# Projections of k and of the first half of q, issued in steps of three matmuls between the indexer's matmuls

## What is computed

```
h = rms_norm(x) * (1 + scale) + shift              # scale, shift from c @ ada_w
z = h @ w_in                                       # columns: u | q | k | v | qi | ki | wi
score = sum_h wi[h] * relu(qi[h] . ki) / const     # indexer, 8 heads of 64; causal
sel = top_k(score, 128 or 130)                     # keys that a query may see
y_att = softmax(q . k[sel] / 8 + bias) @ v[sel]    # 8 heads of 64
y_pool = windowed means of u, minus u, @ pool_w    # 4 groups of 128 channels
x = x + gate * rms_norm([y_pool, y_att] @ w_out)
x = x + gate * rms_norm(relu(h2 @ w_ff1)^2 @ w_ff2)
```

## Time and profile before

| | us |
|---|---|
| median of 3 runs | 950.38 |
| lowest and highest run | 945.65, 954.45 |
| profiled execution, its time | 945.28 |
| profiled execution, its span | 943.4 |
| TensorE busy | 855.5 |
| VectorE busy | 449.0 |
| ScalarE busy | 335.5 |

### The profile page before, as it was taken

One profiled execution on the slowest core, in us unless ns is written; L12 is line 12 of the kernel. 1 busy time (PEld: TensorE's weight loads), 2 busy tenths in 40 slices (PEclk: granted clock), 3 DMA queues, 4 the chain that ended last, 5 costly groups with the idle time before them and its releaser, 6 DMA issues.

```text
span 943.4 us, 11350 instructions
## 1 busy us (share of the span) xinstructions
PE 855.5 (91%) x4136; PEld 645.3 (68%) x4136; DVE 449.0 (48%) x862; ACT 335.5 (36%) x627; POOL 88.1 (9%) x136
## 2 busy tenths in 40 slices
PE   2799889998987986879988999999999999999997
PEld 0477437887844564435766788888888888888875
DVE  0342899778457873231365532234333433344256
ACT  2453642223355563220356332234212331134232
POOL 2141200006123320001010000000000000000000
PEclk9989799999979897999998999999999999999999
DMA  9742300221367566857201222222232222321202
GB/s 323 267 113 83 98 1 11 90 90 64 116 210 265 178 204 203 232 155 237 77 21 50 85 90 90 86 61 77 90 90 67 68 90 89 90 66 69 90 1 100
DMA packets 68777, 105.82 MB, mean 112 GB/s; under 512 B 6986, under 2 KB 32214, under 8 KB 68714
## 3 DMA queue, kind: packets, MB, share of 16 engines
q1 hardware_dynamic: 64194, 96.48, 32.2%
q0 software_dynamic: 3296, 6.39, 2.3%
q10 hardware_dynamic: 1232, 2.23, 0.7%
HBM read 100.04 MB, written 5.15 MB: 112 GB/s over the span
## 4 chain that ended last, share of the span: by engine, by line
PE 72%; DVE 4%; ACT 2%; issue 2%; DMA 1%; SPq 1%; POOL 0%; DVEq 0%; ACTq 0%
PE bank L745 69%; PE bank L748 3%; DVE probs L1789 1%; ACT stage L1228 1%; DMA raw<-in_ada_w 1%; DVE keys L1602 1%; SPq L545 1%; SPq L563 0%; DVE x_res L1890 0%; DVE act_lo L1602 0%; DMA pages<-in_cache_k 0%; POOL near L689 0%; DMA out_k_p<-stage 0%; ACT pv_rows L1228 0%; DVE probs L1804 0%
## 5 line engine op out<-in xcount | busy, mean ns | idle before, releaser
L745 PE MATMUL bank<-act_hi,w_split 128*128 128x512 f32 (+1 forms) x800 | 258.2, 395 | 1.6 <-DVE k_lo L1602 1.6
L745 PEld LDWEIGHTS bank<-act_hi,w_split 128*128 128x128 f32 (+1 forms) x800 | 150.9, 189 | 35.0 <-issue 2.6
L496 DVE TENSOR_TENSOR w_split<-raw,w_split 128x2048 fp32r<-128x2048 f32 (+2 forms) x47 | 105.0, 2236 | 143.0 <-ACT w_split L1203 142.9
L745 PE MATMUL bank<-w_split,hid_hi 128*128 128x512 f32 x512 | 159.2, 392 | 0.0
L745 PE MATMUL bank<-act_lo,w_split 128*128 128x512 f32 (+1 forms) x400 | 156.9, 392 | 0.0
L1203 ACT ACTIVATE w_split<-raw 128x2048 fp32r<-128x2048 f32 (+2 forms) x48 | 89.3, 1862 | 94.7 <-PE bank L745 94.7
L745 PEld LDWEIGHTS bank<-w_split,hid_hi 128*128 128x128 f32 x512 | 95.9, 188 | 20.7
L745 PE MATMUL bank<-w_split,hid_lo 128*128 128x512 f32 x256 | 100.2, 391 | 0.0
L745 PEld LDWEIGHTS bank<-act_lo,w_split 128*128 128x128 f32 (+1 forms) x400 | 75.5, 189 | 15.5
L1228 ACT ACTIVATE stage<-bank 128x512 f32<-128x512 f32 (+3 forms) x51 | 30.1, 591 | 95.5 <-PE bank L745 92.2
L745 PE MATMUL bank<-w_split,act_s 128*128 128x512 f32 (+1 forms) x248 | 60.7, 387 | 1.5 <-DVE out_t L1896 1.5
(11 more groups left out here) (249 smaller groups left out, 1091.9 us busy)
## 6 DMA issues: line engine op xcount, KB each, us to landing
raw<-in_w_ff SPq DMA_DIRECT2D x32, 1024.0 KB, 5.2
raw<-in_ada_w SPq DMA_DIRECT2D x20, 1024.0 KB, 5.2
raw<-in_w_in SPq DMA_DIRECT2D x10, 1024.0 KB, 5.1
pages<-in_cache_k SPq DMA_DIRECT2D x32, 256.0 KB, 3.0
v_pages<-in_cache_v SPq DMA_DIRECT2D x32, 256.0 KB, 3.1
pages<-in_ada_w SPq DMA_DIRECT2D x4, 1024.0 KB, 12.5
raw<-in_w_out SPq DMA_DIRECT2D x4, 1024.0 KB, 6.3
x_in<-in_x_prompt SPq DMA_DIRECT2D x1, 2048.0 KB, 14.6
```

The source lines that it names most:

```text
L496: return ops.tensor_tensor(lo, r, hi.bitcast(F32), ALU.subtract)
L745: return nc.tensor.matmul(out, lhsT, rhs, start=start, stop=stop, skip_group_check=True)
```

## The change

Three pairs of chunks, k0, k1 and q0, are no longer projected by `project` but by a generator `project_steps`, which yields after every three matmuls. TensorE issues four steps of k0 before the prompt's scores and one behind each of the twelve pairs of heads; k1 and q0 are issued in the decode loop, two steps before and two behind each turning of page keys. The pieces' order becomes k0, k1, q0, u0, u1, q1. The scores of every second pair of heads go to banks 6 and 7 in place of 0 and 1. What was between the projections (history, turned channels, turned keys) finds new places, ScalarE and VectorE take the copies, splits and low parts of the three pairs into their indexer code, and VectorE's 36 steps are cut into four times nine with a low part behind each nine.

```diff
-    p += [("qi", 0), ("qi", 1), ("kiwi", 0), ("k", 0), ("k", 1), ("u", 0), ("u", 1)]
-    p += [("q", 0), ("q", 1), ("v", 0), ("v", 1), ("poolw", 0)]
+    p += [("qi", 0), ("qi", 1), ("kiwi", 0), ("k", 0), ("k", 1), ("q", 0), ("u", 0)]
+    p += [("u", 1), ("q", 1), ("v", 0), ("v", 1), ("poolw", 0)]
...
+    for t in range(1, NT):
+        for h in range(H):
+            take(("ix", t, h), (3 if h // 2 % 2 == 0 else 6) + h % 2)
...
-    for t in range(1, NT):
-        for h in range(H):
-            take(("ix", t, h), (3 if h // 2 % 2 == 0 else 0) + h % 2)
...
+    for kind, i in (("k", 0), ("k", 1), ("q", 0), ("u", 0), ("u", 1), ("q", 1)):
+        take((kind, 2 * i), 0), take((kind, 2 * i + 1), 1), take((kind + "R", i), 2), take((kind + "S", i), 2)
+    for g in range(NG):
+        take(("uo", g), 3 + g % 2)
+    for t in range(NT + 1):
+        take(("kout", t), 5 + t % 2)
...
+            def project_steps(kind, i):
+
+                hi, lo, both = piece(kind, i)
+                for j in range(2):
+                    key, cols = (kind, 2 * i + j), slice(128 * j, 128 * j + 128)
+                    out = claim(key)
+                    for kc in range(KC):
+                        mm(out[:, :], hi[:, kc, cols], act_hi[:, kc, :], kc == 0, False)
+                        mm(out[:, :], hi[:, kc, cols], act_lo[:, kc, :], False, False)
+                        last = mm(out[:, :], lo[:, kc, cols], act_hi[:, kc, :], False, kc == KC - 1)
+                        if kc == KC - 1:
+                            done(last, key)
+                            if j == 0:
+                                fold_pending()
+                            else:
+                                done(rows_s(claim((kind + "R", i))[:, :], both), (kind + "R", i))
+                                pending.append((kind, i))
+                        yield
...
+            first_k = project_steps("k", 0)
...
+            steps(first_k, 2)
...
+            steps(first_k, 1)
...
+            steps(first_k, 1)
...
+                    steps(first_k, 1)
...
+            def more_projections():
+                yield from project_steps("k", 1)
+                yield from project_steps("q", 0)
+
+            beside = more_projections()
...
                 done(mm(claim(("ixS", b))[0:64, :], qi_s[:, b, :], kx_t[:, 512 * (b % 2):512 * (b % 2) + 512], True, True), ("ixS", b))
                 done(mm(claim(("ixSn", b))[0:64, 0:DS], qi_s[:, b, :], ki_s[:, b * DS:(b + 1) * DS], True, True), ("ixSn", b))
+                steps(beside, 2)
                 if b + 1 < DB:
                     turn_kidx(b + 1)
+                steps(beside, 2)
                 if b == 0:
...
-            for i in range(2):
-                project("k", i)
-                if i == 0:
-                    pe.wait_ge(S["hist_in"], 16)
-                    out = claim("hist")
-                    for g in range(NG):
-                        last = turn(out[:, 120 * g:120 * g + 120], hist_in[:, 128 * g:128 * g + 128], 120)
-                    done(last, "hist")
+            project("u", 0)
+            pe.wait_ge(S["hist_in"], 16)
+            out = claim("hist")
+            for g in range(NG):
+                last = turn(out[:, 120 * g:120 * g + 120], hist_in[:, 128 * g:128 * g + 128], 120)
+            done(last, "hist")
+            project("u", 1)
...
-            for i in range(2):
-                project("u", i)
-            project("q", 0)
...
+            def first_channels():
+                evacuated(pe, ("u", 1))
+                evacuated(pe, ("uS", 0))
+                for g in range(2):
+                    turn_channels(g)
+
+            project("q", 1, first_channels)
             evacuated(pe, ("u", 3))
             evacuated(pe, ("uS", 1))
-            for g in range(NG):
-                if g == 2:
-                    fold_pending()
+            for g in range(2, NG):
                 turn_channels(g)
             turn_keys()
-            project("q", 1)
...
             act.wait_ge(S["bias_row_out"], 16)
             for t in range(1, NT):
                 L = 128 * (t + 1)
                 for h in range(H):
                     n = (t - 1) * H + h
+                    if n == 10:
+                        k_chunk(0, full(act, ("k", 0)))
                     out = full(act, ("ix", t, h))
                     if n >= 2:
                         act.wait_ge(S["relu_added"], n - 1)
                     free(run(rows[:, n % 2, 0:L], out[:, 0:L], ACT.Relu, scale=HD ** -0.5), ("ix", t, h))
+            k_chunk(1, full(act, ("k", 1)))
+            pair_rows("k", 0)
...
+                if b == 2:
+                    k_chunk(2, full(act, ("k", 2)))
+                    k_tail(0, full(act, ("kS", 0)))
+                if b == 4:
+                    k_chunk(3, full(act, ("k", 3)))
+                    pair_rows("k", 1)
+                if b == 6:
+                    q_chunk(0, full(act, ("q", 0)))
+                    k_tail(1, full(act, ("kS", 1)))
+            q_chunk(1, full(act, ("q", 1)))
+            pair_rows("q", 0)
+            q_tail(0, full(act, ("qS", 0)))
...
+            pair("u", 0, u_chunk, u_tail)
+            free(run(hist_t, full(act, "hist")[:, 0:480].rearrange("p (g n) -> p g n", g=NG)), "hist")
+            pair("u", 1, u_chunk, u_tail)
+            q_chunk(2, full(act, ("q", 2)))
+            for g in range(2):
+                last_rows(g)
+            q_chunk(3, full(act, ("q", 3)))
+            pair_rows("q", 1)
+            for g in range(2, NG):
+                last_rows(g)
             for t in range(NT + 1):
                 r = rows_of(t)
                 n, ins = stage_copy(full(act, ("kout", t))[0:r, :], r)
@@ -1416,7 +1470,7 @@
                 evacuated(act, ("kout", t))
                 store(n, r, heads(o["k_p"][0, 0, 128 * t:128 * t + 128]) if t < NT
                       else o["k_s"][0].rearrange("b t h d -> (b t) (h d)"))
-            pair("q", 1, q_chunk, q_tail)
+            q_tail(1, full(act, ("qS", 1)))
...
+            def k_low(c):
+                dve.wait_ge(S["proj_hi"], 6 + c)
+                free(minus(k_lo[:, c, :], full(dve, ("k", c))[:, :], k_hi[:, c, :]), ("k", c))
+
+            def q_low(c):
+                dve.wait_ge(S["proj_hi"], 10 + c)
+                free(scaled_minus(q_lo[:, c, :], full(dve, ("q", c))[:, :], HD ** -0.5, q_hi[:, c, :]), ("q", c))
+
...
                     n = (t - 1) * H + h
+                    if n == 12:
+                        k_low(0)
...
+            k_low(1)
+            lo_until(AT[("k", 0)] + 3)
...
-            some_rounds(36)
+            some_rounds(9)
+            k_low(2)
+            some_rounds(9)
+            k_low(3)
+            lo_until(AT[("k", 1)] + 3)
+            some_rounds(9)
+            q_low(0)
+            some_rounds(9)
+            q_low(1)
+            lo_until(AT[("q", 0)] + 3)
             free(nc.vector.tensor_copy(score_s[:, 0:PAST], full(dve, "scS")[0:TS, :]), "scS")
             free(nc.vector.tensor_tensor(score_s[:, PAST:LS], full(dve, "scSn")[0:TS, 0:DS], cc("newmask", TS), ALU.add), "scSn")
             evacuated(dve, "scS")
             evacuated(dve, "scSn")
 
 
-            def k_pair(i):
-                for c in (2 * i, 2 * i + 1):
-                    dve.wait_ge(S["proj_hi"], 6 + c)
-                    free(minus(k_lo[:, c, :], full(dve, ("k", c))[:, :], k_hi[:, c, :]), ("k", c))
-                    some_rounds(3)
-                lo_until(AT[("k", i)] + 3)
-
-            def q_pair(i):
-                for c in (2 * i, 2 * i + 1):
-                    dve.wait_ge(S["proj_hi"], 10 + c)
-                    free(scaled_minus(q_lo[:, c, :], full(dve, ("q", c))[:, :], HD ** -0.5, q_hi[:, c, :]), ("q", c))
-                    some_rounds(1)
-                lo_until(AT[("q", i)] + 3)
-
             for i in range(2):
-                k_pair(i)
-            for i in range(2):
+                some_rounds(10)
                 lo_until(AT[("u", i)] + 3)
-                some_rounds(4)
-            q_pair(0)
+            for c in (2, 3):
+                some_rounds(1)
+                q_low(c)
+            lo_until(AT[("q", 1)] + 3)
```

More of the change, by code:

```diff
@@ L205, in plan_banks @@
     take("hist", 5)
-    for kind in ("k", "u", "q"):
-        for i in range(2):
[L208 to L214, removed]
+    for kind, i in (("k", 0), ("k", 1), ("q", 0), ("u", 0), ("u", 1), ("q", 1)):
[4 more added lines that the diff above has]
+        take(("kout", t), 5 + t % 2)
     for t in range(NT + 1):
@@ L840, in _, with project @@
             pending = []
-            def project(kind, i):
+            def project_steps(kind, i):
[15 more added lines that the diff above has]
+                        yield
+            def project(kind, i, between=lambda: None):
                 hi, lo, both = piece(kind, i)
@@ L852, in project @@
                             fold_pending()
+                            between()
                 if i == 0 and kind in ("qi", "w1"):
```

(30 more changed lines are left out.)

10 lines of the change are left out of this document (removed).

## The result

| | median us | range | runs |
|---|---|---|---|
| before | 950.74 | 945.65 to 957.23 | 20 |
| changed | 942.69 | 935.25 to 947.87 | 20 |

What follows compares the result with a forecast made beforehand. VectorE was taken to bound the first pool map: 243.7 us instead of 251.6, 8 us gained, although TensorE gained 11.4 us. With the clock's effect taken as zero, the median 950.4 less 8 gave 942.4 us, range 935 to 953.

Steps and rivals of the forecast that it cites:

- rival D: Beside the prompt scores: steps don't hide, pairs need more than 0.9 us; only 4 us gained, 946; chance 0.20 with B.
- Steps ahead of the scores cost 0: Before the indexer's scores: four steps, 2.7 us, fit into 2.84 us idle; 2.7 us more if the clock falls.
- Beside the prompt scores 18.4 us: Prompt scores: pairs 8.4, twelve steps 8.2 and decode rows 1.8 us make 18.4 instead of 14.4 us.
- Toeplitz wait 1.5 us: Toeplitz stage: third matmul waits for a bank behind ScalarE's added work, 1.5 us lost where 0.67 was.
- Part one: k's first half beside the prompt scores: costs TensorE 4.7 us instead of 12.7, 8.0 us gained.
- Decode turns 5.36 us: Decode scores: each of eight turns takes 2.64 us plus four steps, 5.36 us.
- Part two: k1 and q0 in the decode loop: 3.3 us of the 11.4 us gained on TensorE.
- VectorE's waits 9.2 and 5.6 us: VectorE idles 9.2 us before k's third low part and 5.6 us around k's fourth chunk and u's split.
- TensorE ahead by 2.8 us at the pool map: First pool map: TensorE arrives at 240.9 us and stands 2.8 us for VectorE, which is ready at 243.7.
- Rival A: VectorE isn't the bound; TensorE's 240.9 us holds at the pool map, gain 10.7 to 12 us, time 939; chance 0.26.
- Rival B: Fuller turns, costlier toeplitz wait and turned keys, or a half-clock spell at 122-154 us; gain 0-5, 948; 0.20 with D.
- Rival C: Toeplitz wait through decode turns to 154 us: interleaved small matmuls keep the clock low, loss 31 less 8, about 973; chance 0.05.

Runs made afterwards that it cites:

- experiment 7: Changed kernel with the four steps ahead of the scores issued in one block behind the gap, leaving it open; 947.17 us, ratio 0.9971 to the kernel before.
- experiment 8: experiment 2 with two steps (six matmuls) behind every second pair of heads; 938.33 us, ratio 0.9874 to the kernel before; on another chip 936.17 us, 0.988.
- experiment 6: Changed kernel with k0's 16 steps issued in one go behind the prompt scores, k1 and q0 still in the decode loop; 943.85 us, ratio 0.994.
- experiment 5: Changed kernel with only k0 interleaved; k1 and q0's 32 steps follow the decode loop, VectorE's order fitted; 941.81 us, ratio 0.9928 to the kernel before.
- experiment 3: Changed kernel with nine selection steps moved from before k's third low part to behind the decode scores' reading, lengthening VectorE's wait; 950.96 us, ratio 1.001.
- experiment 2: Changed kernel with VectorE's selection steps dealt out anew to fill its waits, number unchanged; 941.31 us, ratio 0.9897 to the kernel before.

## Why the prediction was right, point by point

Forecast 942.4 us, measured 942.69; forecast gain 8, measured 8.05 (6.2 to 10.6 us by the interval, which leaves out the 4 us of rival D). That close a hit is partly luck: at the landmark the forecast's sum gives 151.9 us, and 154.2 and 153.7 were measured. The original's second profile lay 2.3 us behind its first as well, so the means differ by 7.0.

- **Steps ahead of the scores cost 0, the gap is filled: right.** The first scores come 5.9 us after the bias rows (6.0 before) at clock 1.00. Left open the gap costs 4.4 us at the landmark (experiment 7). There the first scores come 4.8 us later: 2.7 us are the steps' own time, and 2.1 the lower clock. The forecast's bound of 2.7 us was for steps that fill the gap while the clock falls all the same, and no run had that.
- **Beside the prompt scores 18.4 us: the term that was mis-sized.** Pairs took 0.55, 0.73 and 0.895 us (pitches of 1.44, 1.62 and 1.785 less the step), as forecast (0.5, 0.7, 0.9). But a step took 0.89 us instead of 0.68: at a change between 64-row and 128-row matmuls 0.10 us falls on the 128-row side either way (99.38 to 99.71, and 99.94 to 100.27, instead of 0.23). The 0.09 us on the side of the pair were in the forecast without its knowing, since its 0.90 us was read from a pair with 128-row matmuls behind it. Twelve times 0.21 is 2.5 us; the first toeplitz matmul was 2.6 late (27.0 against 24.4). That is rival D's mechanism at a third of its price (D keeps 4 of the 11.4 us), and experiment 8 shows it by halving the number of changes. Under "LDWEIGHTS" the page "TensorE: Matmul & The Clock Gate" of the Trainium skill gives a load of weights its columns over 1.2 in ns, 107 for 128, an estimate of the size of that 0.10 us. In this case's trace the record of such a load lasts 0.19 us, and at both changes it starts together with its matmul (99.38 and 100.27), inside the step 0.22 us ahead of it (99.49 for 99.71). That fits a load that isn't hidden at the change; no run here shows that it is the cause.
- **Toeplitz wait 1.5 us: right** (1.25). Part one was to gain 8.0 us; less 2.5 that is 5.5 at the toeplitz stage (7.1 or 7.6 us late at its end instead of 12.7). With VectorE out of the way it is 6.4 at the landmark (experiment 6, one profile).
- **Decode turns 5.36 us: right** (from 126.77 to 132.24, 5.47). Part two's 3.3 us was half right: 1.7 for the idle in the turns became 1.1 (experiment 5, within the scatter); the 1.6 of the wait at 156.5 us can be had by VectorE's order alone, since experiment 5 lacks it too, and the original's second profile lacked it as well.
- **VectorE's waits 9.2 and 5.6 us: right** (9.3 and 5.4), and so was the length of its chain from the second split to the pool map, 89.6 us forecast, 89.1 measured (157.85 to 247). It only began 2.4 us late, by the term above.
- **TensorE ahead by 2.8 us at the pool map: wrong.** In the first profile it came at 154.0 instead of 149.1 us after the bias rows. At the last decode scores it was 2.9 us late; the wait for q's low part was 1.5 instead of 1.9, but the spell behind it (184 to 188 us, three steps of the stream in 3.56 instead of 2.04 us) cost 1.6; from the turned keys on it needed 26.0 instead of 25.7, with 3.5 lost at half clock instead of 1.6 and the turning as much cheaper. 0.5 us stays unallotted. So "VectorE's number holds" is true when VectorE comes later (experiment 3); when it comes earlier, TensorE's own arrival leaves 3.4 us (experiment 2).
- **Slips in the working**, none of which moves the forecast: 11.4 less 8.0 is 3.4, not 3.3, for part two. The turning of keys by its own terms (5.5 and 1.9) is 7.4, not 7.9; 7.7 was measured. C and half of the other losses are 0.085, not 0.10.
- **Rival A** (10.7 to 12 us) was TensorE's chain without VectorE. Experiment 2 lets it run: 161.0 less 150.6, 10.4 us, at the landmark, and 9.8 us by its ratio. With VectorE's waits in place A's arrival was missed by the steps' 2.5 us, the wait for q's low part and the spells.
- **Rival B**: no spell fell between 122 and 154 us in the changed kernel; the one from 184 us cost TensorE 1.6 us.
- **Rival C**: the turns ran at 1.00. New waits that bring spells were its way in, and that came once in four: the toeplitz wait of 1.25 us brought none in either profile (nor in any of the ten profiles of edited versions), the wait of about 1.5 us for q brought one in the first and none in the second. The spell behind the turned keys, after 1.95 us, was there before too. The rule under "HAM oscillation" on the Trainium skill's page "TensorE: Matmul & The Clock Gate", by which a wait between groups of matmuls can put the clock back, names a risk that these rows bear out in part; a spell for every wait they don't show. The page's own example has waits longer than these.
- **Order behind the pool map unchanged, shift carried whole: right**, as far as a scatter of 5.8 us lets it be seen.

## What to carry to other kernels

Work put into a gap is worth most where the gap is followed by the lower clock: four steps of 48 gave 4 of 8 us. Interleave in larger groups where the neighbours' buffers allow it, because each change of matmul shape had a price here. When two engines arrive within a few microseconds, shortening one gives little (3.4 of 13 us), and lengthening it can cost nearly everything (8.0 of 8.7); look for the one queue order that feeds both, and follow a moved wait to what stands behind it before moving it.

## What the runs showed of the hardware that was not expected

- A step of three 128-row matmuls between 64-row ones takes 0.89 us instead of 0.68, at full clock and with no wait shown. A change between the two costs 0.19 us in all (experiment 8), 0.10 in the step and 0.09 in the scores.
- The clock's spells are not a property of the kernel alone. The gap of 1.65 us was followed by one in all four profiles that have the gap (clock 0.50, for 7 to 10 us). But the original had one from 144 us in its second profile and none there in its first, and the changed kernel one from 184 us in its first and none there in its second.
- The start of attention holds a spell in every profile (clock 0.50 for 6 us or more between 254 and 285 us), whatever came before; what sets it was not tried.
